# Cache pages laid into 32 partitions each, late modulation blocks behind the last key block, two buffers for raw scores

## The reference

```python
mod = jax.nn.silu(c) @ w_ada + b_ada                # (1024 -> 6144), 9 rows: one prompt, eight samples
shift1, scale1, gate1, shift2, scale2, gate2 = jnp.split(mod[:, None, :], 6, axis=-1)
h = rms_norm(x, norm1_g) * (1 + scale1) + shift1
q_a, k_a, v_a, ... = jnp.split(h @ w_in, ...)
q_a = rms_norm(q_a, q_norm_g); k_a = rms_norm(k_a, k_norm_g)
# samples: 2048 cached tokens in 16 pages of 128 (by page_table), 8 heads of 64, and the own 4 tokens
gate = q . mean of each block of 256 keys; the top 3 past blocks and the own block take part
p = softmax(q . k * scale + bias); o_a = p @ v      # prompt: causal, over its own 512 tokens
```

## Time and profile before

| | us |
|---|---|
| three runs | 1416.17, 1418.62, 1430.93 |
| median | 1418.62 |
| profiled execution | 1415.95 |
| its span, first to last instruction | 1414.3 |
| PE busy in the span | 1249.7 (88%) |
| DVE, ACT, POOL busy | 397.1, 236.1, 189.5 |
| moved by DMA | 372.60 MB, mean 263 GB/s |

### The profile page before, as it was taken

The page is one execution under the profiler, slowest core; times in us unless marked ns, Lnnn a source line. Parts: engine busy times, 40 slices in busy tenths (PEclk is TensorE's granted clock), DMA queues, the critical chain, the costliest instruction groups (busy, mean ns, idle before and its releaser), DMA issues.

```text
span 1414.3 us, 17951 instructions
## 1 busy us (share of the span) xinstructions
PE 1249.7 (88%) x6825; PEld 703.2 (50%) x6825; DVE 397.1 (28%) x837; ACT 236.1 (17%) x527; POOL 189.5 (13%) x282
## 2 busy tenths in 40 slices
PE   4989866999999999999999999899778877888886
PEld 2344432445776767688888745533223332333342
DVE  3576923664232423300000034611110011000114
ACT  3121201343232323210000022200000000000002
POOL 2323303320010111110000000111010011000000
PEclk9999988999999999999999999699999999999998
DMA  9968999979243323252110833699999999999985
GB/s 355 338 210 296 324 379 398 386 267 311 86 127 82 116 53 116 53 142 52 62 57 0 319 98 98 223 403 421 423 423 425 425 424 422 423 423 415 425 340 193
DMA packets 116153, 372.60 MB, mean 263 GB/s; under 512 B 10948, under 2 KB 56533, under 8 KB 96622
## 3 DMA queue, kind: packets, MB, share of 16 engines
q1 hardware_dynamic: 93664, 308.96, 56.9%
q0 software_dynamic: 19280, 55.49, 11.7%
q10 hardware_dynamic: 3134, 7.16, 1.6%
HBM read 359.29 MB, written 22.36 MB: 270 GB/s over the span
## 4 chain that ended last, share of the span: by engine, by line
PE 64%; DMA 25%; DVE 6%; issue 2%; ACT 1%; SPq 1%; POOL 0%; POOLq 0%; ACTq 0%; DVEq 0%
PE ps L1637 61%; DMA ring<-in_w_exp_up 19%; PE ps L1648 3%; DVE ring L1127 2%; DMA ring<-in_cache_v 2%; DMA ring<-in_cache_k 1%; DMA ring<-in_w_ada 1%; DMA work<-in_x_prompt 1%; DVE work L1331 1%; SPq L442 0%; DVE work L1626 0%; SPq L466 0%; DVE work L1631 0%; ACT hx L687 0%; DVE hx L1116 0%
## 5 line engine op out<-in xcount | busy, mean ns | idle before, releaser
L1637 PE MATMUL ps<-ring,work 128*64 128x512 f32 (+2 forms) x1856 | 440.7, 624 | 94.8 <-DMA ring<-in_w_exp_up 53.6
L1637 PEld LDWEIGHTS ps<-ring,work 128*64 128x64 f32 (+2 forms) x1856 | 149.7, 143 | 351.0 <-issue 253.8
L1637 PE MATMUL ps<-ring,hx 128*32 128x256 f32 (+3 forms) x1392 | 255.5, 434 | 12.0 <-ACT hx L708 4.3
L1637 PEld LDWEIGHTS ps<-ring,hx 128*128 128x128 f32 (+1 forms) x1392 | 154.2, 154 | 99.1 <-issue 73.9
L1637 PE MATMUL ps<-hx,ring 128*128 128x272 f32 x768 | 179.1, 393 | 0.6 <-DVE work L1331 0.6
L1637 PEld LDWEIGHTS ps<-hx,ring 128*128 128x128 f32 x768 | 145.2, 190 | 31.2 <-DVE work L1331 1.1
L1637 PE MATMUL ps<-work 128*32 128x256 f32 (+10 forms) x850 | 108.4, 359 | 15.4 <-DVE work L1065 8.3
L1637 PE MATMUL ps<-work,ring 128*128 128x272 f32 (+2 forms) x464 | 98.5, 372 | 0.7 <-ACT ring L954 0.7
L1591 DVE TENSOR_TENSOR work<-work,ps 128x256 f32<-128x256 f32 x32 | 13.5, 421 | 279.4 <-ACT work L992 279.4
L1637 PEld LDWEIGHTS ps<-work,ring 128*128 128x128 f32 (+1 forms) x464 | 82.2, 190 | 18.8 <-issue 2.7
L992 ACT ACTIVATE work<-ps 128x256 f32<-128x256 f32 x32 | 12.3, 383 | 433.9 <-PE ps L1637 433.9
(11 more groups left out here) (296 smaller groups left out, 804.0 us busy)
## 6 DMA issues: line engine op xcount, KB each, us to landing
ring<-in_w_exp_down SPq DMA_DIRECT2D x32, 2048.0 KB, 22.7
ring<-in_w_exp_gate SPq DMA_DIRECT2D x31, 2048.0 KB, 18.0
ring<-in_w_exp_up SPq DMA_DIRECT2D x31, 2048.0 KB, 22.6
ring<-in_w_ada SPq DMA_DIRECT2D x12, 2048.0 KB, 15.5
ring<-in_cache_k SPq DMA_DIRECT2D x64, 256.0 KB, 7.6
ring<-in_cache_k POOLq DMA_DIRECT2D x64, 256.0 KB, 6.1
ring<-in_cache_v SPq DMA_DIRECT2D x64, 256.0 KB, 12.3
ring<-in_cache_v POOLq DMA_DIRECT2D x64, 256.0 KB, 6.1
```

The source lines that it names most:

```text
L1637: return pe.matmul(out, lhsT, rhs, start=start, stop=stop, **k)
```

## The change

- **Pages.** A page goes into 32 partitions, four tokens (a row of 8 KB) in each; page q of a block into partitions 32 (q mod 4) and on, in the left or right half of the slot. A transfer has 32 rows in place of 128. For the values a slot then holds four pages of one sequence in a half, two sequences in all, so that products need two slots together: `page_values(u, part)` works on two blocks at once, in two parts, eight products each as before. Scores are folded, and weights turned, with a step of four columns, since a partition's four tokens are neighbours.
- **Modulation blocks 4 to 11** are multiplied in one row behind the last fold and the first turned weights. Blocks 8 to 11 go to PSUM bank 2 in place of 5. ACT copies both results, no longer DVE. `SLOT_ORDER` puts blocks 4 to 8 into five different slots; before, blocks 6 and 7 took the slots of 4 and 5.
- **Raw scores** have two buffers, so ACT's copy waits for the fold before the last one.
- **Order.** DVE lays the queries out before the third key block's transpose and the norm of row tile 3. ACT takes the deviation before the second copy of a step and before the turned rows.

```diff
-        SLOT_ORDER = ([1, 2, 0, 3, 4, 5, 1] + [2, 0, 3, 4, 2, 0, 3, 4, 2, 0, 5, 3, 4, 2, 0, 5] + [3, 4, 3, 4, 1, 2, 0, 3]
+        SLOT_ORDER = ([3, 4, 1, 2, 0, 5, 3] + [4, 1, 2, 0, 4, 1, 2, 0, 4, 1, 5, 2, 0, 4, 1, 5] + [2, 0, 3, 4, 1, 2, 0, 3]
                       + [4, 1, 2, 0, 3] * 3 + [4] + [1, 2, 0, 5, 3, 4] * 3)
...
-            PAGED[("v", i)] = add_block(("v", i), PAGES // 4, (s("pv_s"), i + 1))
+            PAGED[("v", i)] = add_block(("v", i), PAGES // 4, (s("pv_s"), i // 2 + 1))
...
-        key_rows, key_fold = grid(xflat[:, 3072:4096], 4), xflat[:, 4096:4096 + P]
+        key_rows, key_fold = [grid(xflat[:, at:at + 1024], 4) for at in (3072, 2048)], xflat[:, 4096:4096 + P]
+        mod_rows_last = work[:, 1024:1536]
...
-        VALUES_AT = {**{2 * v - 1: v for v in range(1, 8)}, **{2 * v + 4: v for v in range(8, 16)}}
+        VALUES_AT = {**{4 * u - 1 + 2 * part: (u, part) for u in range(1, 4) for part in range(2)},
+                     **{4 * u + 4 + 2 * part: (u, part) for u in range(4, 8) for part in range(2)}}
...
-        ADA_IN = {11: (4, 6), 12: (6, 8), 13: (8, 12)}
...
+        def value_sequence(v, m):
+            return 4 * (v // 8) + 2 * (v % 2) + m
...
             what, i = pieces
             cache = cache_k if what == "k" else cache_v
             for q in which:
-                pg = 8 * i + q
+                m, r = q // 4, slice(32 * (q % 4), 32 * (q % 4) + 32)
                 if what == "k":
                     at = key_sequence(i) * PAGES + 8 * (i // 4 % 2) + q
                 else:
-                    at = (4 * (pg // (4 * PAGES)) + pg % 4) * PAGES + pg // 4 % PAGES
+                    at = value_sequence(i, m) * PAGES + 4 * (i // 2 % 4) + q % 4
                 page = eng.value_load(ptab[0:1, at:at + 1], min_val=0, max_val=cache.shape[1] - 1)
-                src = cache[0, bass.DynSlice(page, 1)].rearrange("a t h d -> (a t) (h d)")
-                eng.dma_start(slot(n)[:, AW * q:AW * q + AW], src).then_inc(sems[SLOT_ORDER[n]], 16)
+                src = cache[0, bass.DynSlice(page, 1)].rearrange("a (b c) h d -> (a b) (c h d)", c=4)
+                eng.dma_start(slot(n)[r, 2048 * m:2048 * m + 2048], src).then_inc(sems[SLOT_ORDER[n]], 16)
...
             act.wait_ge(s("h_ready"), KD // 2)
             def keys_taken(k):
                 act.wait_ge(s("page_sc"), k + 1)
-                if k >= 4:
-                    act.wait_ge(s("fold_ps"), k // 4)
-                act.activation(key_rows[:, k % 4, :], ps[:, 2, 0:256], ACT.Copy).then_inc(s("key_rows"), 1)
+                if k == 4:
+                    act.wait_ge(*after("own_ps"))
+                elif k >= 8:
+                    act.wait_ge(s("fold_ps"), k // 4 - 1)
+                act.activation(key_rows[k // 4 % 2][:, k % 4, :], ps[:, 2, 0:256], ACT.Copy).then_inc(s("key_rows"), 1)
...
-                for k in steps(SCORE_IN, n):
+                for k in steps(SCORE_IN, n)[0:1]:
+                    keys_taken(k)
+                if n < NORMED:
+                    deviations(n)
+                for k in steps(SCORE_IN, n)[1:]:
                     keys_taken(k)
                 if 1 <= n <= NORMED and n != SPQ + 1:
                     turned_rows(n - 1)
-                if n < NORMED:
-                    deviations(n)
...
+            def last_mod_taken(i, bank, rows):
+                act.wait_ge(w_used, i + 1)
+                act.activation(rows, ps[:, bank, :], ACT.Copy).then_inc(s("last_mod_rows"), 1)
+
             weights(0, range(5))
+            last_mod_taken(7, 5, mod_rows)
             exponent(1)
+            last_mod_taken(11, 2, mod_rows_last)
...
                     keys_turned(k)
                 if n < NORMED:
                     variances(n)
-                for k in steps(TURN_IN, n)[1:]:
-                    keys_turned(k)
-                if n < NORMED:
-                    normed(n)
                 if n == SPQ + 1:
                     dve.wait_ge(*after("q_dense"))
                     for k in range(4):
                         last = queries_laid_out(k)
                     last.then_inc(*done("q_blocks"))
+                for k in steps(TURN_IN, n)[1:]:
+                    keys_turned(k)
+                if n < NORMED:
+                    normed(n)
...
-            mod_taken(7)
             softmax_max(1)
-            mod_taken(11)
...
             def ada(i):
@@ -1665,7 +1681,7 @@
                 for q in range(2):
                     k = 2 * (i % 4) + q
                     for j in range(4):
-                        last = mm(ps[32 * j:32 * j + 32, 5, :], cT[:, k, :], w[:, q, 512 * j:512 * j + 512], k == 0, k == KD - 1,
+                        last = mm(ps[32 * j:32 * j + 32, 2 if i >= 8 else 5, :], cT[:, k, :], w[:, q, 512 * j:512 * j + 512], k == 0, k == KD - 1,
...
                 for x in range(2):
-                    out = ps[:, (3, 7)[x], :].rearrange("p (g i b) -> p i g b", g=4, i=4)
+                    out = ps[:, (3, 7)[x], :].rearrange("p (i b c) -> p i c b", i=4, c=4)
                     for i in range(4):
                         for j in range(4):
-                            last = mm(out[32 * j:32 * j + 32, i], key_fold[:, 32 * i:32 * i + 32], key_rows[:, j, P * x:P * x + P], True, True,
+                            last = mm(out[32 * j:32 * j + 32, i], key_fold[:, 32 * i:32 * i + 32], key_rows[f % 2][:, j, P * x:P * x + P], True, True,
                                       skip_group_check=True)
...
                     normed_turned(n - 1)
-                if n < QKV_TILES:
-                    for i in steps(ADA_IN, n):
-                        ada(i)
             keys_folded(3)
-            mod_turned(7)
-            for i in steps(ADA_IN, QKV_TILES):
-                ada(i)
-            pe.wait_ge(s("v_ready"), 5)
-            pe.wait_ge(s("qk_T"), NORMED)
...
                     else:
                         for page in range(4 * q, 4 * q + 4):
-                            last = turn(ps[:, 6 if g else (6, 1)[q % 2], P * (page % 4):P * (page % 4) + P], logits[g][:, P * page:P * page + P])
+                            last = turn(ps[:, 6 if g else (6, 1)[q % 2], P * (page % 4):P * (page % 4) + P],
+                                        logits[g][:, 512 * q:512 * q + 512].rearrange("p (b c) -> p c b", c=4)[:, page % 4, :])
                     last.then_inc(s("pr_tr"), 1)
...
-            def page_values(v):
-                g, i = v // (PAGES // 2), v % (PAGES // 2)
-                if i == 0:
+            def page_values(u, part):
+                g, i = u // 4, u % 4
+                if i == 0 and part == 0:
                     pe.wait_ge(s("pr_T"), 5 * g + 5)
                     if g:
                         pe.wait_ge(s("o_rows"), g)
                     for j in range(4):
                         mm(ps[32 * j:32 * j + 32, 0, :], pr_own[0:NS, 32 * j:32 * j + 32], v_tok[0:NS, PT, :], True, False,
                            skip_group_check=True)
-                n = PAGED[("v", v)]
-                landed(pe, n)
-                for page in (2 * i, 2 * i + 1):
+                n = [PAGED[("v", 2 * u + m)] for m in range(2)]
+                if part == 0:
+                    landed(pe, n[0])
+                    landed(pe, n[1])
+                for c in range(2 * part, 2 * part + 2):
                     for j in range(4):
-                        q = 4 * (page % 2) + j
-                        last = mm(ps[32 * j:32 * j + 32, 0, :], prT[:, page, 32 * j:32 * j + 32], slot(n)[:, AW * q:AW * q + AW],
-                                  False, page == PAGES - 1, skip_group_check=True)
-                last.then_inc(s("pv_s"), 1)
+                        at = 4 * (j % 2) + c
+                        last = mm(ps[32 * j:32 * j + 32, 0, :], prT[:, 4 * i + c, 32 * j:32 * j + 32], slot(n[j // 2])[:, AW * at:AW * at + AW],
+                                  False, i == 3 and c == 3, skip_group_check=True)
+                if part:
+                    last.then_inc(s("pv_s"), 1)
...
+            pe.wait_ge(s("v_ready"), 5)
+            pe.wait_ge(s("qk_T"), NORMED)
             weights_turned(0, range(5))
-            page_values(0)
+            for i in range(FIRST_ADA, 12):
+                ada(i)
+            mod_turned(7)
             mod_turned(11)
+            page_values(0, 0)
+            page_values(0, 1)
             pe.wait_ge(s("mod_set"), 2)
...
                 if x in VALUES_AT:
-                    page_values(VALUES_AT[x])
+                    page_values(*VALUES_AT[x])
```

More of the change, by code:

```diff
@@ L453, in _ @@
                     sp.wait_ge(s("p_tr"), 32)
-                    sp.wait_ge(s("pv_s"), 2 * PAGES // 2)
+                    sp.wait_ge(s("pv_s"), 8)
                 if isinstance(pieces, tuple):
@@ L755, in weights @@
                 if g:
-                    act.wait_ge(s("pv_s"), PAGES // 2)
+                    act.wait_ge(s("pv_s"), 4)
                 for q in part:
@@ L1221, in sample_rows @@
             def sample_rows(g):
```

(10 more changed lines are left out.)

## The result

| | before | changed |
|---|---|---|
| median us | 1417.39 (4 runs) | 1512.69 (4 runs, 1499.02 to 1520.03) |
| ratio | | 1.061, interval 1.054 to 1.067 |
| profiled execution | 1415.95 | 1499.02 |
| its span | 1414.3 | 1497.1 |

The change makes the kernel 6% slower; the prediction had 1405, in a range of 1392 to 1458.

A forecast was written before the change was run, and what follows sets the result against it. From the first cached keys to the attention loop's end, PE bounded first, then DMA, then PE in the loop. Gains 5.5 + 1.6 + 4 - 1.9 + 4.3 = 13.5 us gave a median of 1405.1, range 1392 to 1458.

The forecast's parts named there:

- term (4): Cached-page loads: rows of 8 KB cut a block from 5.43 to 4.95 us, 4.3 us gained over nine blocks.
- the forecast: Whole kernel: 1405 us, own range 1395 to 1413, chance 0.40, half of it on either side of 1404.4.
- the first rival: Page loads into 32 partitions become slow: 1449 us at 270 GB/s, 1487 at 228; chance 0.28.
- pages alternate among four groups of partitions from two queues, which may spread them again: Page loads: a reason why narrow transfers might not stay slow, set against the first rival; no size given.
- Term (1): Before the first key scores: queries laid out earlier remove 3.80 us of wait and half-clock work, 5.5 us gained.
- Term (2): Key blocks: two raw-score buffers and an earlier deviation remove waits of 11.55 and 12.71 us; counted as nothing.
- Term (3): Last fold to values: moved modulation blocks close a DMA dip, 1.6 us, and even the queues, 4 us; against it -1.9.
- the yardstick: Attention loop: time of the third value product, 250.64 before, set by how fast DMA gets through all queued ahead.
- The -1.9 for the pairs: Start of values: the first product, 1.9 us, ran before the second block landed and now needs both blocks.
- some 13 us sooner: Attention loop: sign of a right forecast, the third value product some 13 us sooner than 250.64.
- the same 2.8 us per step: Attention loop: sign of a right forecast, its steps still take 2.8 us each, 35 steps before.
- The fold's output pattern: Score folds: four-word output steps cost 0; rival, doubled cost, 6 us and 1409, lies within the forecast's 0.40.

The follow-up runs named there:

- keys_new: The old layout's run with key pages as in the changed kernel (32 neighbouring partitions, 8 KB rows), value pages in 128 partitions: 1476.85 us, one run.
- queries_first: The kernel before with only the queries laid out on DVE ahead of the third transpose and the norm: 1419.64 us, ratio 0.997.
- the old layout: The changed kernel with pages laid as before (2 KB token in each of 128 partitions), all other parts kept: 1406.67 us, ratio 0.990.
- old_layout_again: The same kernel as the old layout, run again beside a whole kernel with every fourth partition on one chip: 1411.32 us, ratio 0.992.
- long_rows: The old layout's run with each page as 32 pieces of 8 KB in every fourth partition: 1407.09 us, ratio 0.988.
- mods_behind: The kernel before with only modulation blocks 4 to 11 moved behind the last fold, with their slots and banks: 1419.97 us, ratio 0.996.

## Why the prediction was wrong

The step that failed is **term (4)**, "4.95 us per block in place of 5.43", +4.3 us, and with it the choice of the forecast over the first rival. I took the rate of expert weights, which go to 128 partitions, for pages that go to 32, because their rows are as long. At the measured 227 GB/s a block takes 9.2 us, not 4.95. Length of the pieces, on which I sized it, is worth 7% (415 against 387); the partitions, which I left to the rival, cost 41% of the rate (227 against 387).

The reason I gave for not believing the rival was that "pages alternate among four groups of partitions from two queues, which may spread them again". Nothing in the trace said so, and it does not hold: alternating gives 227 GB/s and even queues kept apart 247. The rows against it were on the table: 213 to 254 GB/s for lone loads of 32 rows, and page queues that did not fill up what a narrow transfer leaves. The rate I had in hand was the rate that came: in 90:170 it was 227 GB/s for 32 partitions in a row, 239 for 32 spread over 64, and 247 (9% more than 227) for the queues in different halves, while pages in every fourth partition were fast (345). Why the partitions set the rate, no run shows.

**The first rival** had the right cause, slow pages: 1487 at 228 GB/s, which is 69 us over the median before, where the spans at 227 GB/s differ by 82.8. The count of transfers came out 14 us short, or 16, since its 23 steps of 2.8 us are 64.4 and not 63. What it lacked is the time that PE's work took behind the long waits (16 products in 3.64 us, at a granted clock of 0.50, behind the waits of 10.04 and 10.05 us, where they take 1.92 at full clock), 20.2 us more PE time in the stretch, which a sum of transfers doesn't hold; part of that time is hidden behind transfers, as the two together would be over 82.8. It also took the first five key blocks as free. In five of the runs with slow key pages they were not, as told at `keys_new`, but in the changed kernel's profiled execution no wait shows it.

**Term (1)**, 5.5 us: the 3.80 us of wait and the half clock went as said (in `queries_first` the granted clock was 1.00 in 72:81, where before it was 0.50 in the 3.64 us from 83.36). By itself it gave 4.1.

**Term (2)**, 0: both waits went (with the old layout DVE waits for a deviation 0.4 us at most). What PE gains by that is not known, since this part was not run by itself.

**Term (3)**, 1.6 + 4 - 1.9: without pairs 6.1 measured for 5.6 at the yardstick. The -1.9 for the pairs was not measured. In the changed kernel it was turned round by the slow pages: POOL's value pages run beside SP's last modulation blocks, which then land 13.7 us apart (270.48 and 284.18) where the old layout has 7.3 (207.61 and 214.93) and `keys_new`, with slow keys but values in 128 partitions, 7.5 and 7.2.

**The sum of these**, 5.5 + 1.6 + 4 = 11.1, and "some 13 us sooner" for the third value product with term (4): the old layout has 12.95. That this is so near 13 is luck. The old layout has neither term (4) nor the -1.9, so its count is 11.1, and its second profile (`old_layout_again`) is 11.2 us sooner (239.41). The two parts that ran alone give 4.1 + 6.1 = 10.2. From the loop's end on, gains did pass on nearly one for one (6.5 us there, 7.7 in the spans), but "the same 2.8 us per step" did not hold: from the yardstick to the loop's end it is 89.1 us before and 95.6 with the old layout, and so half of the gain was lost. There the loop met value pages that were not there yet (waits of 1.31 and 0.27 us) and had a stretch at a lower granted clock (0.83 from 270 to 300). The second profile has 95.5 us with no such wait and a clock of 0.50 in 290:300 and 0.88 in 300:310, so the lower clock is enough to take as much.

**The fold's output pattern**: 0 was right. A fold takes 1.95 to 1.96 us at full clock with runs of 32 words in PSUM (before, `old_layout`) and with steps of four words (the changed kernel, `keys_new`); that rival falls.

**The chances**: 0.28 for the slow pages was too little, as all evidence of the trace on this very form of transfer pointed one way and only an analogy the other.

## What to carry to other kernels

Before a transfer is given a new shape, look in the trace for transfers with the same set of partitions, not with the same row length, and believe their rate even if they are few and small. Where loads keep the DMA engines busy all the time, each should be spread over all 128 partitions (pages moved at 384 to 387 GB/s so, and at 212 to 261 in 32 neighbours); every fourth partition does that with the same number of pieces (414 to 417), when the reader of the data can follow. Where DMA bounds a stretch, the sum of slower transfers is not all: in the changed kernel 16 products behind a wait of 6.41 to 10.05 us took 3.64 us in place of 1.92, all five times, at a granted clock of 0.50.

## What the runs showed of the hardware that I had not expected

32 partitions with a step of four were a fast destination: 414 to 417 GB/s in pieces of 8 KB where value pages move (`long_rows`, 230 to 270), faster than 128 partitions in pieces of 2 KB (384 to 387 in the same windows of the old layout).

PE's clock in the attention loop differs between kernels whose loops have the same steps. In 280:310 the granted clock is 1.00 in the kernel before and in `queries_first`, 0.89 and 0.77 in two profiled executions of the old layout, 0.62 in `mods_behind`, though PE has the same two longest idle gaps in its middle, 1.74 and 1.50 to 1.69 us. Value waits do not explain it: the old layout's second execution, at 0.77, had none in its loop. Two of these windows, before and `mods_behind`:

```profile
280.00:310.00 30.00, 26.68 (x163) 14.66 (x162) 16.47 (x52) 11.83 (x34) 5.25 (x11) 1.00 0.72 257
```

```profile
280.00:310.00 30.00, 26.57 (x107) 15.08 (x106) 11.91 (x38) 9.31 (x27) 2.26 (x5) 0.62 0.53 192
```

PE is busy for 26.68 and 26.57 us, with 163 and 107 matmuls. What sets the clock is left open; it is worth as much as the parts of the change that were under test here.
